# Gate rows through a DRAM scratch and a broadcast DMA instead of TensorE transposes, in a two-block transformer kernel

## The reference, cut to what matters

```python
mod = silu(c) @ w_mod + b_mod                 # shift, scale, gate: 1024 values each
# attention layers
y = rms_norm(concat([o_a, o_b]) @ w_out, post_g)
x = x + gate[:, None, :] * y
# feed-forward stages
x = x + 0.5 * gate * swiglu(modulate(x, g, shift, scale), w_in, w_out)
# mixer and spatial gating
x = x + gt * y
```

## Time and profile before

| | before |
|---|---|
| median of 3 runs | 1587.98 us |
| profiled execution, its time | 1587.57 us |
| profiled execution, its span | 1585.7 us |
| PE busy | 1564.3 us, 99% |
| DVE busy | 1172.3 us, 74% |
| ACT busy | 777.9 us, 49% |
| POOL busy | 70.5 us, 4% |
| moved by DMA | 336.97 MB |

### The profile page before, as it was taken

The page is one execution under the profiler, slowest core; times in us unless marked ns, Lnnn a source line. Parts: engine busy times, 40 slices in busy tenths (PEclk is TensorE's granted clock), DMA queues, the critical chain, the costliest instruction groups (busy, mean ns, idle before and its releaser), DMA issues.

```text
span 1585.7 us, 20742 instructions
## 1 busy us (share of the span) xinstructions
PE 1564.3 (99%) x7994; PEld 1296.7 (82%) x7994; DVE 1172.3 (74%) x1917; ACT 777.9 (49%) x1246; POOL 70.5 (4%) x112
## 2 busy tenths in 40 slices
PE   7999999999999999999999999999999999999998
PEld 5787778888888888887777888888888888888887
DVE  7889899759986665477766888868877667666654
ACT  5767666532222222254556555445555463455552
POOL 2000000100000000030010100000000100010000
PEclk9999999999999999999999999999999999999999
DMA  9987676336656655252122777857777685555550
GB/s 378 371 294 275 230 253 222 107 127 231 214 211 239 225 213 176 90 175 80 67 95 74 292 293 289 314 216 266 257 285 269 211 304 188 171 202 188 187 188 33
DMA packets 93044, 336.97 MB, mean 212 GB/s; under 512 B 10625, under 2 KB 11265, under 8 KB 92690
## 3 DMA queue, kind: packets, MB, share of 16 engines
q1 hardware_dynamic: 90706, 327.58, 57.5%
q0 software_dynamic: 2240, 8.06, 1.5%
HBM read 334.56 MB, written 1.05 MB: 212 GB/s over the span
## 4 chain that ended last, share of the span: by engine, by line
PE 55%; DVE 1%; ACT 1%; issue 0%; POOL 0%; POOLq 0%; DVEq 0%; ACTq 0%
PE bank L292 53%; PE bank L295 2%; DVE sb_tm L301 0%; ACT sb_XN L298 0%; DVE sb_X L301 0%; ACT sb_arena L298 0%; ACT sb_XC L298 0%; DVE sb_arena L319 0%; DVE sb_XN L301 0%; DVE sb_sg L316 0%; DVE sb_XC L301 0%; DVE sb_w7r L301 0%; DVE sb_w5r L301 0%; POOL sb_rstd L301 0%; DVE sb_rows L309 0%
## 5 line engine op out<-in xcount | busy, mean ns | idle before, releaser
L292 PE MATMUL bank<-sb_hT,sb_hi 128*128 128x512 f32 (+1 forms) x1856 | 574.9, 379 | 0.0
L298 ACT ACTIVATE sb_hi<-sb_w 128x1024 fp32r<-128x1024 f32 x428 | 431.3, 1052 | 281.8 <-DMA sb_w<-in_w 238.8
L292 PEld LDWEIGHTS bank<-sb_hT,sb_hi 128*128 128x128 f32 x1856 | 332.1, 188 | 58.5 <-issue 0.2
L292 PE MATMUL bank<-sb_hi,sb_hT 128*128 128x512 f32 x1152 | 369.6, 395 | 2.5 <-ACT sb_hT L298 1.3
L292 PEld LDWEIGHTS bank<-sb_hi,sb_hT 128*128 128x128 f32 x1152 | 215.6, 188 | 52.8 <-issue 5.3
L312 DVE CUSTOM_DVE_ANT_0 sb_w<-sb_w,sb_cb 128x1024 f32<-128x1024 f32 x144 | 174.7, 1218 | 0.0
L301 DVE TENSOR_TENSOR sb_sg<-bank,sb_sg 128x512 f32<-128x512 f32 (+1 forms) x90 | 58.9, 660 | 103.1 <-ACT sb_sg L298 82.2
L298 ACT ACTIVATE sb_sg<-bank 128x512 f32<-128x512 f32 (+1 forms) x98 | 55.0, 573 | 118.2 <-PE bank L292 117.7
L298 ACT ACTIVATE sb_arena<-bank 128x512 f32<-128x512 f32 (+1 forms) x106 | 56.4, 559 | 55.4 <-PE bank L292 32.3
L301 DVE TENSOR_TENSOR sb_tm<-bank,sb_rows 128x512 f32<-128x512 f32 (+1 forms) x41 | 28.1, 684 | 69.4 <-PE bank L292 66.5
L298 ACT ACTIVATE sb_XN<-sb_X 128x512 f32<-128x512 f32 x33 | 20.7, 629 | 99.2 <-DVE sb_X L301 91.3
(11 more groups left out here) (483 smaller groups left out, 3209.7 us busy)
## 6 DMA issues: line engine op xcount, KB each, us to landing
sb_w<-in_w SPq DMA_DIRECT2D x428, 512.0 KB, 4.3
sb_w<-in_mw SPq DMA_DIRECT2D x192, 512.0 KB, 4.7
sb_rows<-in_na_rpb POOLq DMA_DIRECT2D x16, 96.0 KB, 3.0
sb_X<-in_x SPq DMA_DIRECT2D x1, 1024.0 KB, 4.9
sb_cb<-in_cvec POOLq DMA_DIRECT2D x2, 512.0 KB, 8.8
sb_XC<-in_ctx POOLq DMA_DIRECT2D x1, 1024.0 KB, 13.0
sb_arena<-in_sg_ln_g POOLq DMA_DIRECT2D x1, 1024.0 KB, 7.1
sb_arena<-in_sg_ln_b POOLq DMA_DIRECT2D x1, 1024.0 KB, 10.4
```

Source lines behind the costliest of these rows:

```text
L292: return self.e.matmul(out, a, b, start=start, stop=stop)
L298: return self.e.activation(out, a, f, **kw)
```

## The change

The gate rows are no longer made on TensorE and ScalarE. `pe_gate` and `act_gate` go, with their eight and two instructions for each of the nine rows. A new function on GpSimd's queue writes the gate's 128 x 8 values from `mods` to a scratch row of 1024 values in DRAM, waits for that transfer and for the last reader of the row `G[...]`, and then reads the DRAM row back with a broadcast to all 128 partitions. The write has 128 pieces of 32 bytes, one for each partition: for this, partition p must hold the values 8p to 8p+7, and so the host puts the columns of the gates' weights, their biases and the post-norm gain in that order. VectorE waits for the load's semaphore where it waited for ScalarE's copy.

```diff
-        def pe_gate(e, target, ring_):
-            e.wait_ge(*modulated(target))
-            for nh in range(2):
-                b = BANK["gate", target, nh] = ring_.take()
-                for f in b.free():
-                    e.wait_ge(*f)
-                for c4 in range(4):
-                    c = nh * 4 + c4
-                    m = e.tr(b.ap[:, c4 * 128:(c4 + 1) * 128], mods[:, TG[target], c:c + 1].to_broadcast([128, 128]), ident)
-                m.then_inc(GBC.sem, GBC.put(target, nh))
-                b.till = ((AE, "gate", target, nh),)
-
-        def act_gate(e, target, g, *after):
...
+        GROW = {"a0": 0, "a1": 1, "m00": 2, "x00": 0, "m01": 1, "m02": 2, "m10": 0, "m11": 1, "m12": 2}
+        gate_rows = nc.dram_tensor("gate_rows", (len(GROW), D), F32).ap()
+
+        def pool_gate(e, stage, *after):
+
+            row, load = gate_rows[list(GROW).index(stage)], LD[f"g{GROW[stage]}"]
+            e.wait_ge(*modulated(stage + "gt"))
+            e.dma(row.rearrange("(p c) -> p c", c=8), mods[:, TG[stage + "gt"], :]).then_inc(
+                LD["row"].sem, LD["row"].put(stage, by=16))
+            for s, *what in after:
+                e.wait_ge(*done(s, *what))
+            e.wait_ge(*done(LD["row"], stage))
+            e.dma(G[GROW[stage]][:, :], row.partition_broadcast(128)).then_inc(load.sem, load.put(stage, by=16))
+
+        def gate_row(stage):
+            return done(LD[f"g{GROW[stage]}"], stage)
...
             def gated(j, nh):
                 e.wait_ge(*done(SQ, p, j, nh))
-                e.wait_ge(*done(AE, "gate", f"a{l}gt", nh))
+                e.wait_ge(*gate_row(f"a{l}"))
...
         def pool_block1(e, l):
+            pool_gate(e, f"a{l}")
             if l == 1:
                 pool_rstd(e, "cx0")
...
                     if s11 == 1 and ns == 2:
                         pe_first_hidden(e, s)
-                    if s11 == b1 - 1 and i == 0:
-                        pe_gate(e, s + "gt", ALLB if ns == 2 else Ring(bank[4:6]))
-                        if ns == 2:
-                            pe_gate(e, "x00gt", ALLB)
...
+            pool_gate(e, "m01", (SMX, "na", 15))
             pool_edge(e, "m02")
...
+            pool_gate(e, "m11", (RES, "mx", 1, 1))
             pool_edge(e, "m12")
...
             pool_block1(e, 1)
+            pool_gate(e, "m00", (MOD, "tile", 47))
+            pool_gate(e, "x00", (RES, 0, 1, 1))
             pool_edge(e, "m01")
             pool_mixer(e)
+            pool_gate(e, "m02", (RES, "m00", 6, 1, 1))
             pool_edge(e, "m10")
+            pool_gate(e, "m10", (SMX, "na", 15), (DE, "mf", 3))
             pool_edge(e, "m11")
             pool_spatial(e)
+            pool_gate(e, "m12", (RES, "m02", 0, 1, 1))
...
+    spread = lambda v: v.reshape(-1, 128, 8).transpose(1, 0, 2).reshape(128, -1)
     for i, kind in enumerate(("sh", "sc", "gt")):
-        put("b" + kind, cols(bias[:, i]))
+        put("b" + kind, (spread if kind == "gt" else cols)(bias[:, i]))
...
+    mw = np.stack([(wide[name][:, c::8] if name[-2:] == "gt" else wide[name][:, c * 128:(c + 1) * 128]).T
+                   for name, c, _ in MT])
```

More of the change, by code:

```diff
@@ L465, in build @@
         LD = {k: signal("load_" + k) for k in ("cb", "cb2", "cst", "cst2", "vec", "x", "pos", "xc", "blk", "small", "mlm", "nb0", "nb1", "nb2", "nb3",
-                                                "sg", "fg", "out")}
+                                                "sg", "fg", "out", "row", "g0", "g1", "g2")}
         slot_load = [signal(f"slot{i}") for i in range(NSLOT + NARENA + NCTX + NXC)]
@@ L960, in build @@
                 {3: ("q", 0), 7: ("k", 0), 11: ("v", 0), 15: ("q", 1), 19: ("k", 1), 23: ("v", 1), 27: ("g", 0), 31: ("g", 1)}]
-        B1 = [{13: [("tq", 0)], 14: [("tk", 0)], 30: [("gated", 0), ("y", 0)], 33: [("gate", 0)]},
+        B1 = [{13: [("tq", 0)], 14: [("tk", 0)], 30: [("gated", 0), ("y", 0)]},
               {6: [("tq", 0)], 9: [("tk", 0)], 29: [("gated", 0), ("y", 0)],
                30: [("cxn", 0)], 31: [("cx", 0)], 32: [("gated", 1), ("y", 1), ("cx", 1)],
[1 row of a table removed]
[1 row of a table added]
         for v in range(6):
@@ L1040, in items @@
                                       lambda c2, k=k, i=i: ((AE, "t" + k, l, i, c2),))
-                    elif what == "gate":
-                        pe_gate(e, f"a{l}gt", HB3)
                     elif what == "cx":
@@ L1337, in act_block1 @@
                                 AE.sem, AE.put("y", l, i, q))
-                    elif what == "gate":
-                        act_gate(e, f"a{l}gt", G[l])
                     elif what == "cx":
@@ L1614, in build @@
         NEXT = {"m00": "m01", "m02": "m10", "m10": "m11", "m12": "fin"}
-        GROW = {"m00": 2, "x00": 0, "m02": 2, "m10": 0, "m12": 2, "m01": 1, "m11": 1}
         def up_tile(s, b0, s11, k):
@@ L1961, in dve_gated @@
             e.wait_ge(*end)
-            e.wait_ge(*done(AE, "gate", gate, nh))
+            e.wait_ge(*gate_row(gate))
             e.wait_ge(DE, DE.n)
@@ L2059, in act_ffn @@
                     act_hidden(e, s, s11)
[L2060 to L2063, removed]
                 for nh in range(2):
@@ L2071, in act_ffn @@
             act_edge(e, NEXT[s], tail, (s, 6 if ns == 2 else 0), (1,), rows_turned(s), hT_free(NEXT[s]))
-        def gate_row_free(s):
-            return {"m00": [(MOD, "tile", 47)], "m02": [(RES, "m00", 6, 1, 1)], "m10": [(SMX, "na", 15), (DE, "mf", 3)],
-                    "m12": [(RES, "m02", 0, 1, 1)]}[s]
         def hT_free(s):
@@ L2150, in dve_context_tail @@
             key = ("d", "m00", 6, 1)
-            dve_residual(e, XC, G[0], "x00gt", BANK[key][2:4], [ended(*key, 2 + j) for j in range(2)], 1,
+            dve_residual(e, XC, G[0], "x00", BANK[key][2:4], [ended(*key, 2 + j) for j in range(2)], 1,
                          ("dm", "m00", 6, 1, 1), ("ctx", 6))
@@ L2198, in build @@
         MX.setdefault(29, []).append(("y", 0))
-        MX[31] += [("gate", 0), ("y", 1)]
+        MX[31] += [("y", 1)]
         def turned(kind, half):
@@ L2269, in pe_mixer @@
                         pe_neighbours(e, i)
-                    elif what == "gate":
-                        pe_gate(e, "m01gt", HB3)
             for j in range(2):
@@ L2708, in act_mixer @@
                         act_neighbours(e, i)
-                    elif what == "gate":
-                        act_gate(e, "m01gt", G[1], (SMX, "na", 15))
                     elif what == "y":
@@ L2841, in residual @@
             def residual(j, nh):
-                dve_gated(e, G[1], "m01gt", BANK["mo", nh][j], ended("mo", nh, j), nh, j, ("dm", "mx", nh))
+                dve_gated(e, G[1], "m01", BANK["mo", nh][j], ended("mo", nh, j), nh, j, ("dm", "mx", nh))
                 dve_total(e, X, nh, j, ("dm", "mx", nh), ("mx",))
@@ L3026, in dve_spatial @@
                 if u == 39:
-                    dve_residual(e, X, G[1], "m11gt", BANK["so", 0], [ended("so", 0, j) for j in range(2)], 0,
+                    dve_residual(e, X, G[1], "m11", BANK["so", 0], [ended("so", 0, j) for j in range(2)], 0,
                                  ("dm", "sg", 0), ("sg",))
             def residual(j, nh=1):
-                dve_gated(e, G[1], "m11gt", BANK["so", 1][j], ended("so", 1, j), 1, j, ("dm", "sg", 1))
+                dve_gated(e, G[1], "m11", BANK["so", 1][j], ended("so", 1, j), 1, j, ("dm", "sg", 1))
                 dve_total(e, X, 1, j, ("dm", "sg", 1), ("sg",))
@@ L3131 @@
     bias = np.concatenate([a["b_ada"].reshape(2, 3, 1024), a["b_mod_2"].reshape(6, 3, 1024)])
+    spread = lambda v: v.reshape(-1, 128, 8).transpose(1, 0, 2).reshape(128, -1)
     for i, kind in enumerate(("sh", "sc", "gt")):
-        put("b" + kind, cols(bias[:, i]))
+        put("b" + kind, (spread if kind == "gt" else cols)(bias[:, i]))
     put("gain", cols(np.concatenate([a["pre_norm_gain"], a["norm_g_2"].reshape(6, 1024)])))
-    put("post", cols(a["post_norm_gain"]))
+    put("post", spread(a["post_norm_gain"]))
     put("bs", a["sg_b_s_2"][0].T)
@@ L3145 @@
             for m in ms for j, s in enumerate(stages) for i, k in enumerate(("sh", "sc", "gt"))}
-    mw = np.stack([wide[name][:, c * 128:(c + 1) * 128].T for name, c, _ in MT])
+    mw = np.stack([(wide[name][:, c::8] if name[-2:] == "gt" else wide[name][:, c * 128:(c + 1) * 128]).T
+                   for name, c, _ in MT])
     rpb = np.pad(a["na_rpb_2"][0][:, 4:11, :], ((0, 0), (0, 0), (48, 48)))
```

14 lines of the change are left out of this document (2 added, 12 removed), and 2 rows, old and new, of the table B1.

## The result

Median after 1582.34 us (1582.06 to 1583.08, 7 runs), before 1587.68 us (1587.47 to 1588.07, 7 runs beside it). The ratio is 0.9967 with a 95% interval of 0.9957 to 0.9976: 5.3 us faster. The forecast was 1582.5. It was counted from a first median of 1587.98 us; against the 1587.68 of the seven runs the measured gain is 5.3 us. The profiled execution took 1582.34 us, with a span of 1580.5.

What follows compares the result with a forecast made beforehand. PE, 99% busy, was taken to set the time nearly everywhere. Profiled 1587.57 us less 5.3 (five places gain, three give nothing, additions cost 0) gives 1582.3; with the median 0.4 above profiled, forecast 1582.5 us, chance 0.68, range 1580.0 to 1586.0.

Steps and rivals of the forecast that it cites:

- PE is the bound, and a transpose is worth its place in the stream: At m00, m02, m10, m11 and m12 the time the transposes take from PE's stream comes back: 1.75 + 4 x 0.88 = 5.27 us.
- Rival D: Each transpose costs its full 272 ns: 48 x 0.27 = 13.1 us, giving 1574.5 us; chance 0.01.
- Nothing at a0, a1, m01: PE soon waits there for work independent of the gate: gain 0, bounds 0 and 0.88 (a0, a1), 0.0 to 0.1 (m01).
- ACT's copies count for nothing: At m00, m02, m10, m11, m12 losing two copies (1.09 us a pair) grows the splits' cover; m01 gains 0.0 to 0.1 us.
- The added waits cost nothing: Write 3.0 us, read 3.7; tightest at m01, 18.5 us for the read, 14.8 to spare; cost 0.
- the upper end of 8.8: Longest landing allowed for each write or read, in us, from broadcasts on full queues; at m01 it leaves 9.7 to spare.
- The weights: Nine reads add 4.7 MB; weight tiles can be 1.7 us late at 40 to 156 us, covered by the splits' lead: 0.
- The banks of m00: Banks in m00 are dealt differently, those of an older tile, free earlier; PE shows no wait there now: 0.

## Why the prediction was right

- **PE is the bound, and a transpose is worth its place in the stream.** Eight were priced at 0.88 us and sixteen at 1.75 from the distance of starts; at the second matmul m00 gave 1.73 and m02 0.88 (from 1.88 just ahead, at 999.89 us in the kernel before, to 2.76), and m10, m11 and m12 gave 0.87, 0.88 and 0.87. Rival D, 272 ns each, would have been 13.1 us.
- **Nothing at a0, a1, m01.** The three have the waits foretold: 1.05 (forecast 1.1), 1.65 (1.6), and 0.77 at m01 (0.9). The kernel with those rows alone through DRAM gave nothing, which is the direct test. This was the step that could have been 2.6 us wrong; it came from looking at the late partner's own input, and not at PE's share.
- **ACT's copies count for nothing.** Shown for this order of the work by the transposes without copies, 1587.71. With the hole at a1 closed they would have counted: PE waits 0.42 us for them there.
- **The added waits cost nothing.** Right for the waits, though the read took 5.3 us (median) and not 3.7; 7.6 was seen at m01 in the run with a late read, still under the upper end of 8.8. That run shows that the 18 us at m01 carry the result. What the prediction did not see is that each DMA on POOL's queue lengthens its closing `DRAIN` by 0.08 us: the eighteen used up 1.5 us of room at the end of the program, and 0.1 us of them shows.
- **The weights.** Cost 0 was right for pieces of 32 bytes. But the argument was about bytes (4.7 MB more, 1.7 us at 312 GB/s), and the run with pieces of 4 bytes shows that the pieces of the write are what can hurt: the same 4 KB in 1024 pieces cost 12.7 us. The prediction took 3.0 us for the write from loads of 96 KB, which say nothing of that. It had the right answer there with half of the reason.
- **The banks of m00.** Priced at 0; they gave 0.1 to 0.2 us. In the kernel before, PE's timeline at 612 us reads

```profile
611.94 0.50 PE L292 MATMUL bank<-sb_hi,sb_gTm006h 128*128 128x512 f32 x1
612.28 0.40 PE L292 MATMUL bank<-sb_w3r,sb_gTm006h 128*128 128x512 f32 x1
```

a distance of 0.34 instead of 0.23, and after the change there is none of over 0.23 at that place. The prediction had said that PE shows no wait there; the list of waits shows none, but the distance does. Likely it is a bank that is freed just in time; no run tested it. At the end of the span some 0.1 us of the shift of 5.39 is missing: POOL's `DRAIN`, which ends 0.1 us behind SyncE's now and ended 1.4 us ahead of it before.

## What to carry to other kernels

Before you count an instruction taken out of the bounding engine, go to its place and follow that engine to its next wait: if one follows within a few microseconds and its partner doesn't depend on what you took out, the gain there is zero; price the rest by the distance of starts, and not by durations. A hole like that is worth a look in itself: here one moved entry on the late engine gave 2.1 us more, and another gave nothing, since that engine was itself full. For a DMA that is off the path, count its pieces as well as its bytes, look at what other queues must have landed meanwhile, and look at the end of the program, where its queue is drained.

## What the runs showed of the hardware that I had not expected

- A write of 4 KB to DRAM in 1024 pieces of 4 bytes was under way for 9.7 to 16.3 us, and while it was, weight tiles of the other queue moved at 36 GB/s where the changed kernel has 323 (891 to 901 us), with a DMA share of 0.20. In 128 pieces of 32 bytes it landed in 3.4 us (median) and held up nothing that shows.
- POOL's closing `DRAIN` took 2.89, 3.38, 3.86, 4.36 and 6.56 us in kernels with 27, 33, 39, 45 and 72 DMAs on its queue, 0.08 us for each. With 72 it set the end of the program, 2.3 us behind SyncE's.
- With the stall of PE of 10.65 us the granted clock fell to 0.50 (1.2 GHz) and stayed there for the first 5.1 us of full work behind it; PE lost 2.0 us in them beyond the stall. After shorter waits, where PE was busy for 1.41 of 4.00 us (100 to 104), it was 0.57 as a mean over the next 4 us of full work.
